# A fused two-block network on one Trainium2 core: parts of one attention between the projection's k-steps every four instead of every five, and the recurrence's preparation two tiles forward

## The reference, cut to what matters

```
h = rms_norm_2(x, norm_mix)
p = h @ w_in                       # 1536 attention columns, 1792 of the RWKV group
sb_q, sb_k, sb_v, rw_in = split(p)
o_sb = rms_norm_2(stick_breaking_attention(rms_norm_2(q), rms_norm_2(k), v))
#   A[t,s] = beta_ts * prod_{s<j<t} (1 - beta_tj), s < t ; 8 heads of 64
u = rw_in + (shift(rw_in) - rw_in) * mu         # 512 r, 512 k, 512 v, 64 w, 64 a, 128 g
log_w = -softplus(-(w0 + tanh(x_w) @ w2)) - 0.5 ; decay = exp(-exp(log_w))
a = sigmoid(a0 + x_a @ a2) ; g = sigmoid(x_g) @ g2
kk = x_k * k_k, normalized by head ; kf = x_k * (1 + (a - 1) * k_a)
S_t = S_{t-1} diag(w_t) + (S_{t-1} a_t) b_t^T + v_t k_t^T ; y_t = S_t r_t   # a_t = -kk, b_t = kk * a
bonus = sum(r * kf * r_k) * v
x = x + concat([o_sb, (norm(y) + bonus) * g]) @ w_out
```

## Time and profile before

| | us |
|---|---|
| runs | 1993.13, 1993.29, 1999.71 |
| median | 1993.29 |
| the profiled execution, its own time | 1992.02 |
| its span | 1989.9 |
| its mean granted TensorE clock | 0.971 of full |

### The profile page before, as it was taken

How to read it: one execution, slowest core, us unless ns; L and a number is a source line. 1 busy time by engine, 2 the same in 40 slices (tenths; PEclk the granted TensorE clock), 3 DMA queues, 4 the chain that set the end, 5 groups by cost and what they waited for, 6 DMA issues and landing times. The chain is left out here.

```text
span 1989.9 us, 27544 instructions
## 1 busy us (share of the span) xinstructions
PE 1854.4 (93%) x11644; PEld 1427.3 (72%) x11644; DVE 874.4 (44%) x1393; ACT 681.2 (34%) x1046; POOL 136.6 (7%) x109
## 2 busy tenths in 40 slices
PE   5899988979999999899999988999789899999999
PEld 2566655758888886688888866665588578888887
DVE  5266776364334344533333343244755543333332
ACT  3225446343223233322122324466322342212221
POOL 0013434200000002000000010000000010000000
PEclk8999999989999999999999999999899899999999
DMA  9672110112222222123123212111000122322230
GB/s 378 214 249 101 33 28 32 54 45 104 95 96 96 95 96 85 53 97 126 64 99 109 99 53 85 53 43 44 21 4 4 54 84 96 115 86 85 96 132 38
DMA packets 44474, 176.13 MB, mean 89 GB/s; under 512 B 5568, under 2 KB 5824, under 8 KB 41024
## 3 DMA queue, kind: packets, MB, share of 16 engines
q1 hardware_dynamic: 44352, 174.38, 24.9%
HBM read 168.33 MB, written 2.10 MB: 86 GB/s over the span
## 5 line engine op out<-in xcount | busy, mean ns | idle before, releaser
L344 PE MATMUL bank<-hs,wsp 128*128 128x512 f32 x1368 | 554.7, 405 | 21.2 <-DVE hs L1541 11.5
L1050 ACT ACTIVATE wsp<-ring 128x1024 fp32r<-128x1024 f32 (+2 forms) x244 | 268.7, 1104 | 842.6 <-PE bank L346 840.6
L345 PE MATMUL bank<-hs,wsp 128*128 128x512 f32 x1368 | 539.7, 395 | 0.0
L346 PE MATMUL bank<-hs,wsp 128*128 128x512 f32 x1368 | 539.4, 394 | 0.0
L1502 DVE TENSOR_TENSOR wsp<-ring,wsp 128x1024 fp32r<-128x1024 f32 (+2 forms) x244 | 312.0, 1281 | 421.8 <-ACT wsp L1050 421.7
L344 PEld LDWEIGHTS bank<-hs,wsp 128*128 128x128 f32 x1368 | 261.0, 191 | 102.9 <-issue 41.2
L345 PEld LDWEIGHTS bank<-hs,wsp 128*128 128x128 f32 x1368 | 261.5, 191 | 55.8 <-issue 3.6
L346 PEld LDWEIGHTS bank<-hs,wsp 128*128 128x128 f32 x1368 | 260.8, 191 | 56.0
L346 PE MATMUL bank<-hids,wsp 128*128 128x512 f32 x608 | 241.3, 397 | 0.0
L345 PE MATMUL bank<-hids,wsp 128*128 128x512 f32 x608 | 241.3, 397 | 0.0
L344 PE MATMUL bank<-hids,wsp 128*128 128x512 f32 x608 | 241.2, 397 | 0.0
(11 more groups left out here) (313 smaller groups left out, 1800.4 us busy)
## 6 DMA issues: line engine op xcount, KB each, us to landing
ring<-m_gate SPq DMA_DIRECT2D x44, 512.0 KB, 3.4
ring<-m_up SPq DMA_DIRECT2D x44, 512.0 KB, 3.4
ring<-m_down SPq DMA_DIRECT2D x32, 704.0 KB, 4.1
ring<-m_w_in SPq DMA_DIRECT2D x38, 512.0 KB, 3.5
arena<-ada_late SPq DMA_DIRECT2D x16, 1024.0 KB, 5.9
ring<-m_w_up SPq DMA_DIRECT2D x32, 512.0 KB, 3.4
ring<-m_w_down SPq DMA_DIRECT2D x32, 512.0 KB, 3.4
ring<-m_w_out SPq DMA_DIRECT2D x16, 512.0 KB, 3.6
```

Source lines behind the costliest of these rows:

```text
L344: pe.matmul(out, lhs[0], rhs[0], start=start, stop=False)
L345: pe.matmul(out, lhs[0], rhs[1], start=False, stop=False)
L346: return pe.matmul(out, lhs[1], rhs[0], start=False, stop=stop)
L1050: act.activation(wsp[:, s % SPLIT, 0, 0:size], ring[:, i % RING, 0:size], ACT.Copy)\
```

## The change

The tiles are projected in another order (k, then w/a and g, then r and v), with the host's layout of the weights in the same order. The parts come every four k-steps. Everything from the rates to the factors is called for two tiles earlier, `first_products` follow in tiles 9 to 12, and the bonus product leaves `first_products` and is called behind the turned values. Its input r * kf * r_k is written over the key tile instead of in `rk`. VectorE's first `wkv_pairs` goes ahead of the last token mix.

```diff
-        rk, kfs, csum = area(32 * K, (2, T)), area(36 * K, (2, T)), area(40 * K, (T,))
+        kfs, csum = area(36 * K, (2, T)), area(40 * K, (T,))
-        RW_ORDER = [12, 13] + list(range(4, 8)) + list(range(0, 4)) + list(range(8, 12))
+        RW_ORDER = list(range(4, 8)) + [12, 13] + list(range(0, 4)) + list(range(8, 12))
+        STEP = 4
@@ TensorE
-            def first_products(c):
+            def bonus(c):
                 pe.wait_ge(S("rkr"), c + 1)
                 claim(2 + c % 2, "bonus", c + 1)
-                pe.matmul(bank[:, 2 + c % 2, :], const("pair"), rk[:, c % 2, :], start=True, stop=True)\
+                pe.matmul(bank[:, 2 + c % 2, :], const("pair"), u[:, UK + c, :], start=True, stop=True)\
                   .then_inc(S("bonus_full"), 1)
+
+            def first_products(c):
                 pe.wait_ge(S("wkv_in"), c + 1)
                 wkv_pairs(0, 0, (6, 7), (c,))
                 first_power(0, (4, 5), (c,))
...
-                    if (8 * n + k) % 5 == 4 and 8 * n + k < 5 * (PARTS + 1):
-                        sb_step((8 * n + k + 1) // 5)
-                    if (n, k) == (8, 4):
+                    if (8 * n + k) % STEP == STEP - 1 and 8 * n + k < STEP * (PARTS + 1):
+                        sb_step((8 * n + k + 1) // STEP)
+                    if (n, k) == (6, 7):
                         osb_ms(3)
-                    if (n, k) == (9, 3):
+                    if (n, k) == (7, 3):
                         rates(0)
                         rates(1)
-                if 4 <= n < 8:
-                    kk_ms(n - 4)
-                if n == 9:
+                    if (n, k) == (12, 3):
+                        bonus(0)
+                        bonus(1)
+                    if (n, k) == (13, 5):
+                        turn_values(2)
+                if 2 <= n < 6:
+                    kk_ms(n - 2)
+                if n == 7:
                     rates(2)
                     rates(3)
+                if 9 <= n < 13:
+                    first_products(n - 9)
                 if n == 11:
                     turn_values(0)
                     turn_values(1)
-                    first_products(0)
-                if n == 12:
-                    turn_values(2)
-                    first_products(1)
             turn_values(3)
-            first_products(2)
-            first_products(3)
+            bonus(2)
+            bonus(3)
@@ ScalarE (sb_step and rates(0), rates(1) as on TensorE; "shifted" counts follow the tile order)
+                if n == 13:
+                    turned_values(2)
                 ahead("w_in2", 8 + n, ("w_in2", 21))
...
+                if 1 <= n < 5:
+                    kk_squares(n - 1)
                 if 3 <= n < 7:
-                    kk_squares(n - 3)
-                if 5 <= n < 9:
-                    kk_root(n - 5)
-                if n == 8:
+                    kk_root(n - 3)
+                if n == 6:
                     osb_root(3)
...
-                if n == 9:
+                if n == 7:
                     rates(2)
                     rates(3)
...
                     key_line(0)
                     decays(0)
                     key_line(1)
+                if 8 <= n < 11:
+                    decays(n - 7)
+                if 8 <= n < 10:
+                    key_line(n - 6)
                 if n == 11:
                     turned_values(0)
                     turned_values(1)
-                    decays(1)
-                    key_line(2)
-                if n == 12:
-                    turned_values(2)
-                    decays(2)
-                    key_line(3)
             turned_values(3)
-            decays(3)
@@ VectorE (sb_step as on TensorE)
+                if n == 13:
+                    wkv_pairs(0, 0, (6, 7))
                 ahead("w_in2", 8 + n, ("w_in2", 21))
                 token_mix(n)
-                if 4 <= n < 8:
+                if 2 <= n < 6:
...
-                if n == 8:
+                if n == 7:
                     dve.wait_ge(S("sb_pv"), PARTS)
                     for c in range(4):
...
-                if n == 9:
                     osb_norm(3)
-                    scan(0)
-                    keys(0)
-                if n == 10:
-                    decayed(0)
-                    scan(1)
-                    keys(1)
-                if n == 11:
-                    decayed(1)
+                if 8 <= n < 12:
+                    decayed(n - 8)
+                if 7 <= n < 11:
+                    scan(n - 7)
+                    keys(n - 7)
+                if n == 12:
                     bonus(0)
-                    scan(2)
-                    keys(2)
-                if n == 12:
-                    decayed(2)
+                if n == 13:
                     bonus(1)
-                    scan(3)
-                    keys(3)
-            decayed(3)
+            do(dve.memset(St[:, :, :, :], 0.0))
             bonus(2)
-            do(dve.memset(St[:, :, :, :], 0.0))
             bonus(3)
...
-            wkv_pairs(0, 0, (6, 7))
             first_power(0, (4, 5))
```

More of the change, by code:

```diff
@@ L1308, in kk_squares @@
             def kk_squares(c):
-                act.wait_ge(S("shifted"), 3 + c)
+                act.wait_ge(S("shifted"), 1 + c)
                 act.activation(u[:, UV + c, :], u[:, UK + c, :], ACT.Square, scale=vec("rw_k_k", c)).then_inc(S("kk_sq"), 1)
@@ L1368, in _ @@
                                scale=unmixed[:, RW_ORDER[n]:RW_ORDER[n] + 1]).then_inc(S("u_raw"), 1)
+                if 1 <= n < 5:
+                    kk_squares(n - 1)
                 if 3 <= n < 7:
-                    kk_squares(n - 3)
-                if 5 <= n < 9:
-                    kk_root(n - 5)
-                if n == 8:
+                    kk_root(n - 3)
+                if n == 6:
                     osb_root(3)
-                    act.wait_ge(S("shifted"), 1)
+                    act.wait_ge(S("shifted"), 5)
                     act.activation(u[0:DH, UWA, :], u[0:DH, UWA, :], ACT.Tanh).then_inc(S("tanh"), 1)
-                if n == 9:
+                if n == 7:
                     rates(2)
                     rates(3)
-                    act.wait_ge(S("shifted"), 2)
+                    act.wait_ge(S("shifted"), 6)
                     act.activation(u[:, UG, :], u[:, UG, :], ACT.Sigmoid).then_inc(S("wa"), 1)
@@ L1897, in keys @@
                 do(dve.tensor_tensor(kf, kf, u[:, UK + c, :], ALU.mult))
-                dve.scalar_tensor_tensor(out=rk[:, c % 2, :], in0=u[:, UR + c, :], scalar=vec("rw_r_k", c), in1=kf,
+                dve.scalar_tensor_tensor(out=u[:, UK + c, :], in0=u[:, UR + c, :], scalar=vec("rw_r_k", c), in1=kf,
                                          op0=ALU.mult, op1=ALU.mult).then_inc(S("rkr"), 1)
@@ L1916, in decayed, with wkv_pairs @@
                 own("wkv_in")
+            def wkv_pairs(w, xx, banks):
+                dve.wait_ge(S("pairs_full"), 4 * (w // 2) + 2 * xx + w % 2 + 1)
+                for e in range(2):
+                    dve.tensor_tensor(AT[w % 2][:, 2 * xx + e, :], bank[:, banks[e], :], const("chunk4"), ALU.mult)\
+                       .then_inc(S("pairs"), 1)
+                    own("pairs")
             def bonus(c):
@@ L1925, in _ @@
                 for k in range(KD):
-                    if (8 * n + k) % 5 == 4 and 8 * n + k < 5 * (PARTS + 1):
-                        sb_step((8 * n + k + 1) // 5)
+                    if (8 * n + k) % STEP == STEP - 1 and 8 * n + k < STEP * (PARTS + 1):
+                        sb_step((8 * n + k + 1) // STEP)
+                if n == 13:
+                    wkv_pairs(0, 0, (6, 7))
                 ahead("w_in2", 8 + n, ("w_in2", 21))
                 token_mix(n)
-                if 4 <= n < 8:
-                    dve.wait_ge(S("kk_ms"), n - 3)
-                    dve.tensor_scalar(u[:, UV + n - 4, :], bank[:, 7, :], 1e-24, None, ALU.max).then_inc(S("kk_max"), 1)
-                if n == 8:
+                if 2 <= n < 6:
+                    dve.wait_ge(S("kk_ms"), n - 1)
+                    dve.tensor_scalar(u[:, UV + n - 2, :], bank[:, 7, :], 1e-24, None, ALU.max).then_inc(S("kk_max"), 1)
+                if n == 7:
                     dve.wait_ge(S("sb_pv"), PARTS)
@@ L1963, in heads4 @@
                 return v.rearrange("p (c t) -> p c t", c=4)
[L1965 to L1970, removed]
             def first_power(w, banks):
@@ L2262, in lay_out @@
     w2 = f["w_in_2"][0]
-    u = w2[:, 1536:].reshape(D, 14, P)[:, [12, 13] + list(range(4, 8)) + list(range(4)) + list(range(8, 12))]
+    u = w2[:, 1536:].reshape(D, 14, P)[:, list(range(4, 8)) + [12, 13] + list(range(4)) + list(range(8, 12))]
     mats["w_in2"] = tiles(np.concatenate([w2[:, 0:1024], u.reshape(D, -1)], 1))
```

## The result

The changed kernel takes 1997.0 us in the median of 20 runs; the kernel before, run beside it, 1992.4 us. The ratio is 1.0032 (1.0019 to 1.0044), some 6.4 us slower (the medians alone differ by 4.7), within what the prediction calls no change. The profiled execution took 1996.22 us, its span is 1994.4 us. The page's first part answers to the earlier trace rows; no engine did more or less.

The account below looks back on a forecast made before the run. TensorE, 93% busy, was taken as the bound, with some 23 us of idle time and low clock as the ceiling. 1992.02+4.0+1.8 gave 1997.8 us profiled, 1999.1 us as the median forecast; range 1994 to 2004 (0.68).

Parts of the forecast that it names:

- The new waits: TensorE at `first_products`, waiting for VectorE's factors: idle 3.4, 1.4 and 2.9 us; also `kk_ms` behind ScalarE's logarithm.
- the loop of 9.0 us: Tiles after the rates: decays, key line, split on ScalarE, then VectorE's subtract to scan, setting 9.0 us between scans.
- leg 1: From the attention's first part to the first rates' matmul: parts every four k-steps cost +4.0 us.
- (a) to (d): Leg 1's terms: part 1 +0.7; parts 6 and 12 +1.1, +0.8; `kk_ms` waits +1.7, +0.9; rates -1.2 us.
- The clock's step: TensorE's low clock: 1.2 us charged behind idle time at tile 10, turn(1) and turn(3), nothing behind 0.8 to 1.7 us waits.
- R: The first rates' matmul on TensorE, the border between the two legs, from which leg 2's times are counted.
- leg 2: From the first rates' matmul to the second `key_values`: two tiles moved forward cost +1.8 us.
- step (c): `kk_ms` directly behind `osb_ms` on one bank waits for ScalarE's logarithm: +1.7 us at part 6, +0.9 at part 12.
- leg 2's bounds: No low clock behind turn(1) and turn(3): -2.5 us; VectorE never waiting in the loop: -2.1; together -2.8.

Follow-up runs that it names:

- e2: Changed kernel with each attention part one k-step later, still every four k-steps; ratio 0.9997 to the kernel before.
- e1: Kernel before with only the parts moved to every four k-steps instead of five; ratio 1.0027 to the kernel before.
- e3: Changed kernel with VectorE's four knorm products behind token mix 6 instead of token mix 7; ratio 1.0003 to the kernel before.
- e8: Kernel before with turn(1) and turn(2) one tile later on TensorE, ScalarE's copies of turned values moved to match; ratio 0.9958 to the kernel before.
- e4: Changed kernel with each `first_products` one tile later and VectorE's first pair products behind the loop; ratio 1.0032 to the kernel before.
- e7: Changed kernel with parts one k-step later, knorm behind token mix 6, scan(c) ahead of decayed(c-1), and bonus(1) in tile 12; ratio 0.9992 to the kernel before.
- e5: Changed kernel with VectorE's scan(c) ahead of decayed(c-1); ratio 1.0029 to the kernel before.
- e6: Changed kernel with each `kk_ms` behind the next tile's second k-step, apart from `osb_ms`; ratio 1.0014 to the kernel before.

## Why the prediction was right

The forecast was 1997.8 us for the profiled execution, +5.8 us; the ratio gives +6.4 us (3.8 to 8.8), and the profiled execution +4.2 us, with a stage that began 2.2 us earlier (in spans: -2.2 ahead of the stage, +7.9 in it, -1.2 behind it). The new waits and the loop of 9.0 us are what was forecast. That the total comes so near is in part luck: the stage lost 2.1 us more than the 5.8 of the sum, all of it in leg 1. By its steps:

- (a) to (d) of leg 1 said 8.7 us of idle time (1.3+0.7, 1.1, 1.7, 0.8, 0.9 and 2.2); the trace has 1.97, 1.00, 1.26, 0.78, 1.13 and 2.53, in sum 8.7. The term that was missing is the clock in part 1. The clock's step put "nothing behind the 0.8 to 1.7 us waits" and had no charge for part 1's, which grew to 1.97 us: the stretch behind it ran at 0.74, and leg 1's busy time is 2.0 us more than in e2, where that wait is 1.29 us and the clock 1.00. So leg 1 came out at +6.3 for +4.0.

```profile
1272.00:1277.00 5.00, 5.00 (x19) 3.74 (x17) 1.38 (x2) 2.74 (x4) 0.00 (x0) 0.74 0.00 0
```

- The first scan at R+12.0 (start; I had its end at +14.9, low clock counted, so the start at +13.7) comes 1.7 us sooner than forecast, because TensorE did not fall to a low clock at the rates. From there every step fits: scans 9.0 us apart, idle 3.1, 1.2 and 2.8 us at `first_products` (3.4, 1.4, 2.9 forecast), 2.3 at turn(1) (2.9), 2.5 at turn(3) (2.3). The second `key_values` stands at R+75.8, forecast 76.0: the clock's gain at the rates and its losses behind turn(1) (0.51 there) and turn(3) (0.50) nearly cancel, which is luck too: the sum charged 1.2 us for each, and all six variants have the full clock behind turn(3).

```profile
1414.50:1425.00 10.50, 8.18 (x37) 6.50 (x38) 6.92 (x12) 2.81 (x5) 0.00 (x0) 0.51 0.01 2
```

- The sum hid one thing that the runs showed. e1 alone is 5.4 us slower and the whole change 6.4: the rest of the change, the two tiles forward above all, cost little (1.6 us by the stage, 1.8 forecast), but it also bought nothing, since it left the loop of scans in place and put knorm ahead of it (e3: 3.1 us at the first scan, 1.8 at turn(1)). And the idle time of before at turn(1) was not a lag of VectorE that an earlier start cures: e8 takes it away by letting tile 12 go ahead of the turn, and ScalarE's exps ahead of its copy.
- Small slips in the working changed nothing: 7.6 less 2.0 us is a tile of 5.6, not 5.5, which shifts 0.2 us between the legs and leaves their sum; and step (c) adds up to 5.1, not 5.2. The "together -2.8" of leg 2's bounds does not follow from its -2.5 and -2.1.
- The rule on TensorE's clock in the Trainium skill ("TensorE: Matmul & The Clock Gate", section "What's actually happening"), taken for each new wait, would have put 6 us more on the sum. The trace has the full clock (1.00) in the 5 us behind the waits of 0.8 to 1.3 us at parts 6 and 12, so the strict reading fails, but low ones behind 1.97 us (0.74) and around turn(1) (0.51); my own charge, made for idle times from 2.02 us on, fits these except part 1, where I had left it out. It does not fit the rates: 2.53 us of idle time, and 1.00 behind it.

## What to carry over

When work of another kind is placed between the steps of a loop that several engines follow, its phase against the loop's end counts more than its density: one k-step later was worth 5.2 us of leg 1 here (some 7 by the runs) at the same spacing, because the other engines' work at a tile's end no longer stood ahead of the part's own. A wait in the trace names the instruction that shows a bound, not the one that sets it: move the instruction (e4), and if the wait moves with it, look in the chain for the loop, here one through two other engines. And before starting a chain earlier, ask whether the stalled instruction must stand where it does: moving two turns and their copies one tile later gave 8.4 us where the whole change had cost 6. Last, compare two traces at the point that the edit acts on, and not over a whole stretch, when the clock behind it differs between them.

## What was not expected of the hardware

The granted clock after the same idle time differs from kernel to kernel. All eight traces of the changed kernel and its variants (e2 to e7) have 2.53 us idle at the rates, with the same instructions behind it; the two traces of the changed kernel agree with each other. The next 4.9 us ran at 1.00 in four of them (both of the changed kernel, e3, e5) and at 0.65 or 0.66 in the other four (e2, e4, e6, e7):

```profile
1372.97:1377.87 4.90, 4.90 (x14) 2.31 (x15) 0.00 (x0) 2.72 (x4) 0.00 (x0) 0.66 0.00 0
```

and the same stretch of the changed kernel:

```profile
1375.40:1380.30 4.90, 4.84 (x20) 2.87 (x20) 0.00 (x0) 3.61 (x6) 0.00 (x0) 1.00 0.00 0
```

It moved the first scan by 1.6 us (R+12.0 to R+13.7). At turn(3) the same was seen, the other way round: behind 2.52 us of idle time the next 2.5 us ran at 0.50 in both traces of the changed kernel and at 1.00 in e2, e3, e5 and e6. The changed kernel's row and e3's:

```profile
1438.62:1441.12 2.50, 2.50 (x6) 1.50 (x7) 0.39 (x1) 0.60 (x1) 0.00 (x0) 0.50 0.00 0
1440.62:1443.12 2.50, 2.50 (x12) 1.02 (x14) 1.09 (x2) 0.60 (x1) 0.00 (x0) 1.00 0.00 0
```

That made 1.4 us of leg 2. Which of the two clocks follows was not to be read from the length of the idle time. The clock at the rates also bears on the stages above: e2, e4, e6 and e7 carry some 1.6 us of it in leg 2 ahead of the first scan, e3 and e5 don't. What decides it was not tried.
